# Keys' mean of squares in two fp32r passes at the end of v's unit, queries' mean beside the values, v scaled ahead of the reciprocals

## What is computed

```python
qkv = (xn @ w_qkv).reshape(B, L, 3, N_HEADS, HEAD_DIM)
q = rmsnorm(qkv[:, :, 0], gq)
k = rmsnorm(qkv[:, :, 1], gk)
v = qkv[:, :, 2]
...
s = jnp.where(col_mask[:, None, :], sc + bias, -jnp.inf)
p = jax.nn.softmax(sc, axis=(-2, -1))
```

## Time and profile before

| | |
|---|---|
| median of 3 runs | 1833.74 us |
| profiled execution, its own time | 1835.04 us |
| its span in the trace | 1833.2 us |
| TensorE (PE) busy | 1823.1 us, 99% |
| VectorE (DVE) busy | 1361.2 us, 74% |
| ScalarE (ACT) busy | 827.1 us, 45% |
| GpSimd (POOL) busy | 300.1 us, 16% |
| one pair in the middle of attention | 25.16 us |

### The profile page before, as it was taken

How to read it: one execution, slowest core, us unless ns; L and a number is a source line. 1 busy time by engine, 2 the same in 40 slices (tenths; PEclk the granted TensorE clock), 3 DMA queues, 4 the chain that set the end, 5 groups by cost and what they waited for, 6 DMA issues and landing times.

```text
span 1833.2 us, 26257 instructions
## 1 busy us (share of the span) xinstructions
PE 1823.1 (99%) x9996; PEld 1562.0 (85%) x9996; DVE 1361.2 (74%) x2120; ACT 827.1 (45%) x1357; POOL 300.1 (16%) x239
## 2 busy tenths in 40 slices
PE   9999999999999999999999999999999999999999
PEld 7888988978888988989889898897777788989889
DVE  7686866978866768768767686687887666858657
ACT  6343443643343433435434343465666543434433
POOL 0310401223102104012031130211111003104011
PEclk9999999999999999999999999999999999999999
DMA  5244235532222322346323223642222232322354
GB/s 189 75 144 121 92 116 153 127 121 72 93 103 86 122 92 92 116 133 166 115 70 115 93 100 107 169 127 88 77 74 86 70 115 75 133 92 92 115 150 126
DMA packets 75420, 201.81 MB, mean 110 GB/s; under 512 B 14665, under 2 KB 27626, under 8 KB 75307
## 3 DMA queue, kind: packets, MB, share of 16 engines
q1 hardware_dynamic: 54784, 178.28, 28.3%
q0 software_dynamic: 6912, 12.59, 3.9%
q10 hardware_dynamic: 13610, 9.41, 1.9%
HBM read 185.57 MB, written 3.93 MB: 103 GB/s over the span
## 4 chain that ended last, share of the span: by engine, by line
PE 92%; DVE 5%; issue 1%; ACT 1%; DMA 0%; SPq 0%; DVEq 0%; ACTq 0%
PE bank L1522 25%; PE bank L1524 25%; PE bank L1523 25%; PE bank L1473 5%; PE bank L1476 4%; PE bank L1477 4%; PE bank L1735 1%; PE bank L1726 1%; DVE t L1063 1%; DVE wlr L487 1%; DVE x L1242 0%; DVE wlr L510 0%; PE bank L1745 0%; PE bank L1715 0%; PE bank L1751 0%
## 5 line engine op out<-in xcount | busy, mean ns | idle before, releaser
L1522 PE MATMUL bank<-xh,whr 128*128 128x512 f32 x1408 | 551.1, 391 | 0.7 <-DVE wlr L487 0.5
L1523 PE MATMUL bank<-xl,whr 128*128 128x512 f32 x1408 | 548.6, 390 | 0.0
L1524 PE MATMUL bank<-xh,wlr 128*128 128x512 f32 x1408 | 548.6, 390 | 0.0
L478 ACT ACTIVATE whr<-rest 128x512 fp32r<-128x512 f32 (+1 forms) x445 | 273.6, 616 | 456.5 <-PE bank L1524 444.6
L487 DVE TENSOR_TENSOR wlr<-rest,whr 128x512 fp32r<-128x512 f32 (+1 forms) x445 | 326.8, 738 | 118.2 <-ACT whr L478 115.7
L1522 PE MATMUL bank<-hsh,whr 128*128 128x256 f32 x1232 | 349.5, 284 | 1.1 <-DVE x L1242 0.9
L1523 PE MATMUL bank<-hsl,whr 128*128 128x256 f32 x1232 | 348.6, 283 | 0.0
L1524 PE MATMUL bank<-hsh,wlr 128*128 128x256 f32 x1232 | 348.6, 283 | 0.0
L1522 PEld LDWEIGHTS bank<-xh,whr 128*128 128x128 f32 x1408 | 264.8, 188 | 58.7 <-issue 2.1
L1523 PEld LDWEIGHTS bank<-xl,whr 128*128 128x128 f32 x1408 | 264.9, 188 | 55.5 <-issue 1.0
L1524 PEld LDWEIGHTS bank<-xh,wlr 128*128 128x128 f32 x1408 | 264.7, 188 | 55.1
(11 more groups left out here) (201 smaller groups left out, 2138.6 us busy)
## 6 DMA issues: line engine op xcount, KB each, us to landing
rest<-in_ffn_w_gate SPq DMA_DIRECT2D x61, 512.0 KB, 3.7
rest<-in_ffn_w_up SPq DMA_DIRECT2D x61, 512.0 KB, 4.6
rest<-in_ffn_w_down SPq DMA_DIRECT2D x54, 512.0 KB, 4.5
raw_area<-in_ffn_w_gate SPq DMA_DIRECT2D x26, 512.0 KB, 3.8
raw_area<-in_ffn_w_up SPq DMA_DIRECT2D x26, 512.0 KB, 4.7
raw_area<-in_ffn_w_down SPq DMA_DIRECT2D x26, 512.0 KB, 4.5
raw_area<-in_w_qkv SPq DMA_DIRECT2D x24, 512.0 KB, 3.5
raw_area<-in_w_in_ab SPq DMA_DIRECT2D x16, 512.0 KB, 3.5
```

The costliest lines, as they stand in the source:

```text
L478: act.activation(whr[:, at:at + st.kb, :].rearrange("p k c -> p (k c)"), weights(st, buf)[:, 0, :], ACT.Copy).then_inc(high, 1)
L1522: pe.matmul(out, whr[:, at, :], hi, start=start, stop=False, skip_group_check=onto)
L1523: pe.matmul(out, whr[:, at, :], lo, start=False, stop=False, skip_group_check=onto)
L1524: return pe.matmul(out, wlr[:, at, :], hi, start=False, stop=stop, skip_group_check=onto)
```

## The change

Keys' squares get a high part `sqkh` (ScalarE, behind `probs_t(1)`) and a low part `sqkl` (GpSimd, `square_low`), the block matrix an fp32r copy `headr` (once, ScalarE, in pair 0). `key_mean` becomes two fp32r passes, and moves behind v's unit. `query_mean` takes its place ahead of k = 5 behind `first_values`, and writes bank 2 (bank 6 in pair 0), so that it no longer waits for keys' mean; `turn(3)`, which writes bank 2 too, waits until ScalarE has read it. ScalarE takes the queries' square root ahead of the keys'. VectorE scales v ahead of both reciprocals. `turn_values` waits for the keys' square root, which is now the last reader of bank 3. The diff, without the new semaphores and tiles:

```diff
@@ scalar, attention
                     act.wait_ge(evac, ph.group(p, 1) + 1 + EVAC_CREDIT)
+                    if attends:
+                        act.wait_ge(sqkl_done, p)
                     act.activation(sqk[:, :], kt[:, :], ACT.Square).then_inc(sqk_done, 1)
                 if attends and projects:
                     probs_t(0)
                     probs_t(1)
+                if projects:
+                    act.wait_ge(sqk_done, p + 1)
+                    if attends:
+                        act.wait_ge(k_mean, p)
+                    else:
+                        act.wait_ge(heads_done, 4)
+                        act.activation(headr[:, :], heads[:, :], ACT.Copy).then_inc(headr_done, 1)
+                    act.activation(sqkh[:, :], sqk[:, :], ACT.Copy).then_inc(sqkh_done, 1)
...
                 if projects:
+                    act.wait_ge(q_mean, p + 1)
+                    act.activation(rq[:, :, :],
+                                   bank[2 if attends else 6][:, 0:2 * TT].rearrange("p (t h) -> p t h", t=TT), ACT.Sqrt,
+                                   bias=cst[:, C_EPS:C_EPS + 1]).then_inc(q_std, 1)
                     act.wait_ge(k_mean, p + 1)
                     act.activation(rk[:, :], bank[3][:, :], ACT.Sqrt, bias=cst[:, C_EPS:C_EPS + 1]).then_inc(k_std, 1)
                     if attends:
                         act.wait_ge(s_mm, 4 * p)
                     act.activation(qh[:, :], qt[:, :], ACT.Copy).then_inc(qh_done, 1)
-                    act.wait_ge(q_mean, p + 1)
-                    act.activation(rq[:, :, :], bank[3][:, 0:2 * TT].rearrange("p (t h) -> p t h", t=TT), ACT.Sqrt,
-                                   bias=cst[:, C_EPS:C_EPS + 1]).then_inc(q_std, 1)
                     split_high(act, *ahead(ph, p, 2, last))
@@ vector, attention
-                    dve.wait_ge(k_std, p + 1)
-                    dve.reciprocal(rk[:, 0:SEQ], rk[:, 0:SEQ]).then_inc(rk_done, 1)
                     if attends:
                         dve.wait_ge(v_mm, p)
                     scaled(ph, p, 2, vt[:, :], unit_bank(ph, p, 2))
+                    dve.wait_ge(k_std, p + 1)
+                    dve.reciprocal(rk[:, 0:SEQ], rk[:, 0:SEQ]).then_inc(rk_done, 1)
                     dve.reciprocal(rk[:, SEQ:TOK], rk[:, SEQ:TOK]).then_inc(rk_done, 1)
@@ tensor, attention
                 def key_mean():
-                    pe.wait_ge(sqk_done, p + 1)
-                    pe.wait_ge(heads_done, 4)
+                    pe.wait_ge(headr_done, 1)
+                    pe.wait_ge(sqkl_done, p + 1)
                     if attends:
                         pe.wait_ge(vs_done, p)
-                    pe.matmul(bank[3][:, :], heads[:, :], sqk[:, :], start=True, stop=True).then_inc(k_mean, 1)
+                    pe.matmul(bank[3][:, :], headr[:, :], sqkh[:, :], start=True, stop=False)
+                    pe.matmul(bank[3][:, :], headr[:, :], sqkl[:, :], start=False, stop=True).then_inc(k_mean, 1)
 
                 def query_mean():
                     pe.wait_ge(sqq_done, p + 1)
-                    pe.wait_ge(k_std, p + 1)
                     for t in range(TT):
-                        last = pe.matmul(bank[3][:, 2 * t:2 * t + 2], sqq[:, t * P:(t + 1) * P],
+                        last = pe.matmul(bank[2 if attends else 6][:, 2 * t:2 * t + 2], sqq[:, t * P:(t + 1) * P],
                                          cst[:, C_HEAD:C_HEAD + 2], start=True, stop=True)
...
                 def turn_values():
                     pe.wait_ge(evac, by["qkv"].group(p - 1, 2) + 1 + EVAC_CREDIT)
-                    pe.wait_ge(q_std, p)
+                    pe.wait_ge(k_std, p)
...
-                    unit(ph, 0, 2, hooks={5: key_mean})
-                    query_mean()
+                    unit(ph, 0, 2, hooks={5: query_mean})
+                    key_mean()
                     return
...
-                unit(ph, p, 2, hooks={1: second_scores, 5: lambda: (first_values(), key_mean())})
-                query_mean()
+                unit(ph, p, 2, hooks={1: second_scores, 5: lambda: (first_values(), query_mean())})
+                key_mean()
                 turn(2)
+                pe.wait_ge(q_std, p + 1)
                 turn(3)
@@ gpsimd
+            def square_low(p):
+                pool.wait_ge(sqkh_done, p + 1)
+                pool.tensor_tensor(sqkl[:, :], sqk[:, :], sqkh[:, :].bitcast(F32), ALU.subtract).then_inc(sqkl_done, 1)
+
...
             mask(0, False)
+            square_low(0)
             low_parts(0)
             with pool.Fori(1, PAIRS) as p:
+                square_low(p)
                 mask(p, True)
                 low_parts(p)
```

More of the change, by code:

```diff
@@ L286, in build_trunk @@
         (wh2, wl2, qt, kt, vt, sqq, sqk, vs, qh, ql, kh, kl, braw, bmask, sc, pt, oh, ol, rsum, nmax, rq,
-         rk) = region([
+         rk, sqkh, sqkl, headr) = region([
             ("wh2", [P, KD, P], F32R), ("wl2", [P, KD, P], F32R), ("qt", [P, TOK]), ("kt", [P, TOK]), ("vt", [P, TOK]),
@@ L292, in build_trunk @@
             ("oh", [P, KD, TOK], F32R), ("ol", [P, KD, TOK], F32R), ("rsum", [P, 2, 2]), ("nmax", [P, 2, 2]),
-            ("rq", [P, TT, 2]), ("rk", [P, TOK])])
+            ("rq", [P, TT, 2]), ("rk", [P, TOK]), ("sqkh", [P, TOK], F32R),
+            ("sqkl", [P, TOK], F32R), ("headr", [P, P], F32R)])
         wh, wl = wh + [wh2], wl + [wl2]
@@ L330, in build_trunk @@
         sqq_done, sqk_done, heads_done = sem("sqq_done"), sem("sqk_done"), sem("heads_done")
+        sqkh_done, sqkl_done, headr_done = sem("sqkh_done"), sem("sqkl_done"), sem("headr_done")
         q_mean, q_std, rq_done, k_mean, k_std, rk_done = (sem("q_mean"), sem("q_std"), sem("rq_done"), sem("k_mean"),
@@ L819, in attention @@
                     probs_t(1)
+                if projects:
[6 more added lines that the diff above has]
+                    act.activation(sqkh[:, :], sqk[:, :], ACT.Copy).then_inc(sqkh_done, 1)
+                if attends and projects:
                     exps(2)
```

## The result

The changed kernel takes 1836.85 us (median of 20 runs, 1835.7 to 1838.85) beside 1833.7 for the kernel before (20 runs): a ratio of 1.0018, 95% interval 1.0012 to 1.0024, so 3.15 us more. That is 2.65 above the forecast: inside the stated range (1831.8 to 1837.2), but past the bounds of the sum itself (1832.4 to 1836.4). The profiled execution took 1837.16 around a span of 1835.4 us.

The account below looks back on a forecast made before the run. PE was taken to bound the kernel, busy 1823.1 of 1833.2 us. Pair 0 +1.0, six middle pairs -1.9 and pair 7 +1.4 gave +0.5 on the median 1833.74: 1834.2 us, range 1831.8 to 1837.2.

Parts of the forecast that it names:

- A middle pair: Pairs 1 to 6 of the attention phase: net gain 0.32 us each, 1.9 us for six.
- the sum's own bounds: Whole kernel: middle pairs gain 0.1 to 0.5 each, each end varies 0.4 either way; 1832.4 to 1836.4 us.
- PE's saving of 0.40 a pair: PE's work in a middle pair falls by 0.40 us, between 0.1 and 0.5.
- V: Start of the first values on PE in a pair, the zero for its times.
- The keys' chain of 7.28, kl at K + 7.47: Square root to end of kl takes 7.28 us; PE asks at K + 8.25, so no wait in middle pairs.
- K: End of the two keys' mean passes behind v's unit on PE, put at V + 4.45 in a middle pair.
- Pair 0's loss of 1.0 and pair 7's of 1.4: PE waits for kl at first scores of pair 1 and the output projection: losses of 1.0 and 1.4 us.
- A wait of 0.08: At second values PE needs the second evacuation at K + 3.32 and has it at K + 3.40: 0.08 us.
- 0.40 later: Second values begin 2.01 us after the unit's start and need the second evacuation 0.40 us after that.
- ScalarE's order holds every pair: Rival, chance 0.06: slower ScalarE steps make PE wait 0.6 us longer at second values, about six times; 1837.8 us.
- The clock in the new waits: Rival, chance 0.03: PE's clock halves after waits at both ends' first scores, 1.8 us each; 1837.8 us.
- v ahead of the reciprocals: VectorE scales v first: ready for PE's next unit at about 1321.4 instead of 1322.3, and 0.54 off the keys' chain.

Follow-up runs that it names:

- e1: Against the changed kernel: both ScalarE evacuations of turned probabilities put directly behind the keys' square root; 1834.3 us, ratio to before 1.0001.
- e4: Against the changed kernel: pair 0 alone put back in the old order, with fp32 keys' mean first; 1836.12 us, ratio to before 1.0012.
- e5: Against the changed kernel: v scaled between the two reciprocals again in pairs with attention; 1850.66 us, ratio to before 1.0088.
- e2: Against the kernel before: only the two fp32r keys' mean passes, at the old place, in pairs 1 to 7; 1833.67 us, ratio 0.9998.
- e3: Against e2: v scaled ahead of both reciprocals in pairs 1 to 6; 1830.94 us, ratio to the kernel before 0.9982.
- e6: Against the changed kernel: only the first evacuation of turned probabilities moved directly behind the keys' square root; 1837.47 us, ratio to before 1.0018.

## Why the prediction was right, and where it was off

The measured time lies in the stated range, but not by the forecast's mechanism. A middle pair was to be 0.32 shorter and came out 0.15 longer; the sum's own bounds, which ended at 1836.4, missed the result, and only what had been added for the rivals took it in. For the middle pairs that is luck; the two ends came as forecast.

- **PE's saving of 0.40 a pair** held as a sum: 0.40 at the next unit, and 24.75 a pair in e1. The two passes stand 0.23 apart and without a gap. To the hundredth it was luck: keys' mean ended at V + 4.56 where I had V + 4.45, and the turns behind it took 0.80 where I had 0.91.
- **The keys' chain of 7.28, kl at K + 7.47** held: K is 1320.90 + 0.23 = 1321.13 and kl ends at 1328.56, K + 7.43. No first scores of a middle pair wait.
- **Pair 0's loss of 1.0 and pair 7's of 1.4** held: 1.01 and 1.44, both released by kl, and e4 takes the first away. At the end part of it (0.96 in the row) now stands at the second values, ahead of the wait for kl (1.16), where I had one wait of 1.8 for kl; the loss of the stretch is the same, since kl ends it.
- **"A wait of 0.08"** is the step that failed. My time for the evacuations was right: the pair ends at 1324.46, K + 3.33, where I had 3.35 before its 0.05 to PE. What failed is when PE needs the second one, "0.40 later": I split a row of eight matmuls into a first and a second half, one head after the other. The heads run together, so the second evacuation was needed at the start. The wait came out as 0.09 for the first evacuation and 0.47 for the second: 0.48 more than the term, in each of six pairs 2.9 us, against a miss of 2.65. Of the 0.48, 0.40 is what I had allowed the second head; most of the rest is that PE reached the next unit at K + 0.80 and not at K + 0.91, and so asked sooner.
- **The rival "ScalarE's order holds every pair"** had the right place and the right size (0.6 a pair) with a chance of 0.06. I gave it the wrong condition, slower ScalarE steps: the steps took what their rows said, and it decided all the same. Its time, 1837.8, was nearer to the measured one than my sum's.
- **The clock in the new waits** did not fall. TensorE behind the first scores that waited 1.78, changed kernel: timeline, then the view of a stretch (from:to, length, busy us of PE, PEld, DVE, ACT and POOL with counts, granted clock, DMA share, GB/s):

```profile
1255.19 0.40 PE L1490 MATMUL bank<-xl,whr 128*128 128x512 f32 x1
1255.43 0.39 PE L1491 MATMUL bank<-xh,wlr 128*128 128x512 f32 x1
```

```profile
1254.80:1257.80 3.00, 3.00 (x16) 2.46 (x14) 2.96 (x6) 2.00 (x4) 0.00 (x0) 1.00 0.72 239
```

The passes stay 0.22 to 0.24 apart, and the granted clock reads 1.00, the 2.4 GHz level. The spacing is the firmer sign: in the opening of the kernel before the clock reads 1.00 too (5.80 to 10.50), with passes 0.43 apart. The rule that an idle PE is put back to half clock (the Trainium skill, TensorE: Matmul & The Clock Gate, section Why this matters for your kernels) did not come into play at waits of this length; no run here shows one at which it does.

- **v ahead of the reciprocals**, which I had costed as free and as 0.54 taken off the chain, turned out to be a condition: without it weight loads wait 2.5 a pair (e5), and 0.43 even with the old order of the means (e2).

## What to carry to other kernels

A row of a timeline that groups instructions can hide two streams that share the array: before a group is given a "first half needs this, second half that", look through a window shorter than one instruction at how many are under way; if several are, take the start of the group as the time at which all their inputs are needed. Moving a small product later on the busiest engine moves all that is queued behind its reader on the reader's engine; here one copy of 0.6 us in that queue decided between the saving and a loss. Where a cheaper form of an operation and a new place for it come in one change, try the form at the old place: e3 kept the saving and left the ends as they were.

## What the runs showed of the hardware that I had not expected

Waits in the middle of TensorE's work, repeated every pair, left its speed alone. In e5 PE stood 2.30 us for v and went on at once at full speed (0.23 a pass):

```profile
1329.11 0.50 PE L1490 MATMUL bank<-xh,whr 128*128 128x512 f32 x1 [2.30 <-DVE vt L987]
1329.45 0.40 PE L1493 MATMUL bank<-xl,whr 128*128 128x512 f32 x1
1329.68 0.39 PE L1494 MATMUL bank<-xh,wlr 128*128 128x512 f32 x1
```

The opening, which the change doesn't touch, differs among the profiles. In that of before, passes of 0.63 stand 0.43 apart until 10.46, and so they do in e5 and e6 until about 10.4 and 10.3; in that of the changed kernel they are 0.23 apart from the start, though the work ahead of them is the same row of 4.21:

```profile
1.61 4.21 PE L1618 MATMUL bank<-small 128*128 128x128 f32 x18 [1.61 <-DVE small L924]
...
6.57 0.39 PE L1537 MATMUL bank<-xl,whr 128*128 128x512 f32 x1
6.80 0.40 PE L1538 MATMUL bank<-xh,wlr 128*128 128x512 f32 x1
```

The first mean of pair 0 comes at 1243.02 after, and at 1244.33 before, 1.31 earlier; such an offset is as large as the terms of the sum, which is why the account above is made of stretches and not of points in time. The spacing alone does not set it: e3, with passes 0.23 apart, comes to that point at 1243.98, and e5, with 0.43, at 1243.64. What sets the opening was not tried, nor whether it goes with the kernel or with the execution, since one execution of each kernel was profiled.
